# A block group of a down projection: k-tiles 12 to 15 split earlier, k-tiles 16 to 19 split later, and sixteen moves spread over the loads

## The reference, cut to what matters

```python
def swiglu(x, w_gate, w_up, w_down):
    return (jax.nn.silu(x @ w_gate) * (x @ w_up)) @ w_down

x = x + 0.5 * swiglu(rms_norm(x, ffn1_norm[layer]), ffn1_w_gate[layer], ffn1_w_up[layer], ffn1_w_down[layer])
```

## Time and profile before

| what | value |
|---|---|
| median of three runs | 2539.7 us |
| the profiled execution, own time | 2539.15 us |
| its span, first to last instruction | 2536.9 us |
| TensorE (PE) busy | 2502.3 us, 99% |
| VectorE (DVE) busy | 2055.7 us, 81% |
| ScalarE (ACT) busy | 1239.9 us, 49% |
| mean granted TensorE clock | 0.998 of full speed |

### The profile page before, as it was taken

How to read it: one execution, slowest core, us unless ns; L and a number is a source line. 1 busy time by engine, 2 the same in 40 slices (tenths; PEclk the granted TensorE clock), 3 DMA queues, 4 the chain that set the end, 5 groups by cost and what they waited for, 6 DMA issues and landing times.

```text
span 2536.9 us, 33755 instructions
## 1 busy us (share of the span) xinstructions
PE 2502.3 (99%) x12499; PEld 2128.4 (84%) x12499; DVE 2055.7 (81%) x2443; ACT 1239.9 (49%) x1692; POOL 254.6 (10%) x284
## 2 busy tenths in 40 slices
PE   8999999999999999999999999999999999999998
PEld 7888988888889888888888888888888888888887
DVE  7988758889888699975566999769988679899874
ACT  6445436664444544543225545445454437654542
POOL 0000004800000000000000000000000047200000
PEclk9999999999999999999999999999999999999999
DMA  6776432156754367553333675545766321367552
GB/s 212 166 166 141 111 96 78 34 150 158 177 114 141 118 167 169 126 137 108 100 97 111 169 167 126 138 141 132 165 135 156 100 90 42 109 157 169 125 142 87
DMA packets 493313, 331.38 MB, mean 131 GB/s; under 512 B 287968, under 2 KB 405472, under 8 KB 493152
## 3 DMA queue, kind: packets, MB, share of 16 engines
q1 hardware_dynamic: 481056, 285.19, 40.2%
q0 software_dynamic: 12096, 44.05, 9.9%
HBM read 248.68 MB, written 2.10 MB: 99 GB/s over the span
## 4 chain that ended last, share of the span: by engine, by line
PE 85%; DVE 8%; ACT 2%; issue 2%; SPq 1%; DMA 1%; POOL 1%; DVEq 0%; POOLq 0%; ACTq 0%
PE pair L594 25%; PE pair L595 25%; PE pair L596 25%; PE pair L801 3%; PE pair L802 3%; PE pair L803 3%; DVE wl L1751 2%; DVE Hl L1763 1%; PE pair L877 1%; ACT wh L1246 1%; SPq L2787 1%; PE pair L953 0%; PE pair L952 0%; DVE Df L1763 0%; DVE Dl L1763 0%
## 5 line engine op out<-in xcount | busy, mean ns | idle before, releaser
L1246 ACT ACTIVATE wh<-raw 128x1024 fp32r<-128x1024 f32 (+4 forms) x571 | 576.5, 1013 | 679.3 <-PE pair L596 534.8
L1751 DVE TENSOR_TENSOR wl<-raw,wh 128x1024 fp32r<-128x1024 f32 (+4 forms) x571 | 662.3, 1163 | 249.7 <-ACT wh L1246 248.0
L594 PE MATMUL pair<-wh,Xl 128*128 128x512 f32 (+2 forms) x976 | 374.9, 384 | 7.4 <-DVE wl L1751 7.3
L594 PE MATMUL pair<-wh,Sl 128*128 128x512 f32 x960 | 373.9, 389 | 1.0 <-DVE wl L1751 0.9
L596 PE MATMUL pair<-wh,Xh 128*128 128x512 f32 (+2 forms) x976 | 373.9, 383 | 0.0
L595 PE MATMUL pair<-wl,Xh 128*128 128x512 f32 (+2 forms) x976 | 373.8, 383 | 0.0
L596 PE MATMUL pair<-wh,Sh 128*128 128x512 f32 x960 | 373.5, 389 | 0.0
L595 PE MATMUL pair<-wl,Sh 128*128 128x512 f32 x960 | 373.5, 389 | 0.0
L1246 ACT ACTIVATE wh<-part 128x1024 fp32r<-128x1024 f32 x144 | 153.0, 1062 | 277.9 <-PE pair L596 91.2
L594 PE MATMUL pair<-Hh,wl 128*128 128x512 f32 (+1 forms) x669 | 257.9, 386 | 0.0
L595 PE MATMUL pair<-Hl,wh 128*128 128x512 f32 (+1 forms) x669 | 257.5, 385 | 0.0
(11 more groups left out here) (347 smaller groups left out, 4341.2 us busy)
## 6 DMA issues: line engine op xcount, KB each, us to landing
raw<-in_ffn_w_gate SPq DMA_DIRECT2D x120, 512.0 KB, 5.4
raw<-in_ffn_w_up SPq DMA_DIRECT2D x120, 512.0 KB, 4.3
raw<-in_ffn_w_down SPq DMA_DIRECT2D x114, 512.0 KB, 4.7
part<-raw POOLq DMA_DIRECT2D x66, 512.0 KB, 5.4
H<-H SPq DMA_DIRECT2D x288, 64.0 KB, 3.9
H<-squares SPq DMA_DIRECT2D x192, 64.0 KB, 2.1
raw<-in_c_w_in SPq DMA_DIRECT2D x24, 512.0 KB, 3.6
raw<-raw POOLq DMA_DIRECT2D x18, 512.0 KB, 9.2
```

The source lines that it names most:

```text
L594: e.matmul(o, ll, rh, start=start, stop=False, skip_group_check=again)
L1246: e.activation(part_of(n, wh), source_of(n), ACT.Copy).then_inc(whi.up(("w", n)), 1)
L1751: e.tensor_tensor(part_of(n, wl), source_of(n), part_of(n, wh).bitcast(F), ALU.subtract).then_inc(wlo.up(("w", n)), 1)
```

## The change

On ScalarE, one copy of k-tiles 12 to 15 of tokens 0 to 255 (1024 values per partition) at p of 8 takes the place of four of 512 values later; D0's high part moves ahead of c6; the high parts of k-tiles 16 to 19 stand behind those of B0 and B1. On VectorE, the low part `Al` of the same block (p of 9) and D0 (p of 11) are made inside the loop over p, D0's low part behind it, all ahead of the wait for batch 5; k-tiles 16 to 19 get their low parts at u of 4 and 5 of the group, and D3 its low part at u of 7. On SyncE, the sixteen moves of batch 5 stood as six ahead of c6's load and ten ahead of c7's; they now stand as four ahead of c6's, two ahead of c7's, and two ahead of each of the group's first five loads.

```diff
+        Al = nc.alloc_sbuf_tensor_at("Al", [128, 4, 256], R, offset=sq_at)
...
-                turned_product(a, "dA", inputs(BLOCKED, 0))
+                turned_product(a, "dA", upper)
...
# ScalarE
+                    if p == 8:
+                        w.wait_ge(mm, ("E2", s, 4))
+                        w.wait_ge(turned_in[3], ("turned", s, 3))
+                        copy(Hh0[:, BLOCKED:BLOCKED + 4, 0:256],
+                             H[:, BLOCKED:BLOCKED + 4, 0:2, :].rearrange("p k t q -> p k (t q)"), ("Ah", s))
+                w.wait_ge(dve, ("D", s, 0))
+                copy(Dh[0][:, :, :], Df[0][:, :, :], ("Dh", s, 0))
                 w.wait_ge(dve, ("h", s, 4))
                 use()
...
-                for j in (0, 3):
-                    w.wait_ge(dve, ("D", s, j))
-                    copy(Dh[j][:, :, :], Df[j][:, :, :], ("Dh", s, j))
-                for k0 in (BLOCKED, BLOCKED + 4):
-                    use()
-                    for k in range(k0, k0 + 4):
-                        hidden_high(s, k)
+                w.wait_ge(dve, ("D", s, 3))
+                copy(Dh[3][:, :, :], Df[3][:, :, :], ("Dh", s, 3))
+                use(2)
+                for k in range(BLOCKED + 4, BLOCKED + 8):
+                    hidden_high(s, k)
# VectorE, in the loop over p
+                    if p == 9:
+                        w.wait_ge(act, ("Ah", s))
+                        w.wait_ge(turned_in[3], ("turned", s, 3))
+                        tt(Al[:, :, :], inputs(BLOCKED, 0), Hh0[:, BLOCKED:BLOCKED + 4, 0:256].bitcast(F), ALU.subtract, ("Al", s))
+                    if p == 11:
+                        w.wait_ge(mm, ("xused", s))
+                        difference(0, inputs(BLOCKED, 0), inputs(BLOCKED, 256))
+                difference_low(0)
...
-                for m in (3, 5):
-                    w.wait_ge(turned_in[m], ("turned", s, m))
-                w.wait_ge(mm, ("xused", s))
+                w.wait_ge(turned_in[5], ("turned", s, 5))
                 difference(2, inputs(BLOCKED, 256), inputs(BLOCKED + 4, 256))
                 difference(1, inputs(BLOCKED, 0), Df[2][:, :, :])
                 for t in range(2):
                     add_down(t)
                 use()
-                difference(0, inputs(BLOCKED, 0), inputs(BLOCKED, 256))
                 difference(3, inputs(BLOCKED + 4, 0), Df[1][:, :, :])
                 use()
-                for j, k0 in ((2, BLOCKED), (1, BLOCKED + 2)):
-                    difference_low(j)
-                    for k in (k0, k0 + 1):
-                        hidden_low(s, k)
-                use()
-                for j, k0 in ((0, BLOCKED + 4), (3, BLOCKED + 6)):
-                    difference_low(j)
-                    for k in (k0, k0 + 1):
-                        hidden_low(s, k)
-                use()
+                difference_low(2)
+                difference_low(1)
+                use()
                 use()
                 for t in range(2, 4):
                     add_down(t)
                 for u in range(14):
+                    if u in (4, 5):
+                        for k in (2 * u - 8, 2 * u - 7):
+                            hidden_low(s, BLOCKED + 4 + k)
+                    if u == 7:
+                        difference_low(3)
# SyncE
-  (3, ((4, 0, 6), (4, 2, 2), (4, 3, 2), (4, 4, 4), (4, 5, 2))), (5, ((4, 6, 6), (4, 7, 10)))):
+  (3, ((4, 0, 6), (4, 2, 2), (4, 3, 2), (4, 4, 4), (4, 5, 2))), (5, ((4, 6, 4), (4, 7, 2), *((4, n, 2) for n in range(8, 13))))):
```

More of the change, by code:

```diff
@@ L772, in blocked, with upper, lower @@
                 a, b, d, x = pairs_of(s)
-                def inputs(k0, q0):
+                def upper(k):
+                    w.wait_ge(act, ("Ah", s))
+                    w.wait_ge(dve, ("Al", s))
+                    return Hh0[:, BLOCKED + k, 0:256], Al[:, k, :]
+                def lower(q0):
+                    k0 = BLOCKED + 4
                     def parts(k):
@@ L810, in blocked @@
                 turned_product(d, "dD", sums(0))
-                turned_product(b, "dB2", inputs(BLOCKED + 4, 256))
-                turned_product(a, "dA2", inputs(BLOCKED + 4, 0), False)
+                turned_product(b, "dB2", lower(256))
+                turned_product(a, "dA2", lower(0), False)
                 turned_product(x, "dE2", sums(3), False)
@@ L1969, in ffn, with inputs, difference, difference_low @@
                                 hidden_low(s, k)
+                def inputs(k0, q0):
+                    return H[:, k0:k0 + 4, :, :].rearrange("p k t q -> p k (t q)")[:, :, q0:q0 + 256]
+                def difference(j, x, y):
+                    w.wait_ge(dve, HERE)
+                    tt(Df[j][:, :, :], x, y, ALU.subtract, ("D", s, j))
+                def difference_low(j):
+                    w.wait_ge(act, ("Dh", s, j))
+                    tt(Dl[j][:, :, :], Df[j][:, :, :], Dh[j][:, :, :].bitcast(F), ALU.subtract, ("Dl", s, j))
                 for p in range(14):
```

## The result

| | us | |
|---|---|---|
| before | 2540.34 (2538.56 to 2541.12, 4 runs) | |
| after | 2577.52 (2574.52 to 2580.11, 4 runs) | ratio 1.0147, 95% interval 1.0129 to 1.0165 |
| forecast | 2546, range 2530 to 2556 | |

The change makes the kernel 37 us slower. The direction and the place were forecast, the size was not: 6 us were expected, and 2577.5 us lies outside the range of 2530 to 2556. The profiled execution after has a span of 2574.6 us, 37.7 more than before.

A forecast was written before the change was run, and what follows sets the result against it. VectorE's order around batch 5 was taken as the bound: 16.4 us of waits and clock go, 15.6 us of stalls and 6.8 us of low clock come, net +6.0 us, so 2546 us, range 2530 to 2556.

The forecast's parts named there:

- The waits at line 801: TensorE's waits at the block group, laid to VectorE's order around batch 5, go: 14.7 us plus 1.7 us of clock.
- The early and the late work is free: VectorE's added early work (3.4 us a stage) fits its idle time, and work moved into the group catches up: costs nothing.
- The stall falls on c6: VectorE ends c6's low part 4.82 us after its wait for batch 5, so a landing after 249.86 stalls TensorE there.
- When the last move lands: Batch 5's last move lands at 252.5 in stage 1, stalling TensorE 2.6 us in each of six stages, 15.6 us.
- the sum (+6.0): Whole kernel: 16.4 us away against 15.6 us of stalls and 6.8 us of low clock added, net +6.0 us.
- a deeper queue pays less per load: SyncE's queue: reason for taking the landing at 252.5, with 2.5 us a round from a span of 2.1 to 3.2.
- rival (c): GpSimd's additions share the DMA engines with batch 5's last moves: stall 3.9 us a stage, +17, 2557 us; chance 0.16.
- The clock: Stalls at c6 lower TensorE's granted clock in four of six stages, 1.7 us each, 6.8 us.
- a landing at 255.0: Batch 5's last move in stage 1 if each round of load and two moves takes 3.2 us, the upper end.
- the addition's 3 us: Upper bound on what one GpSimd addition sharing the DMA engines could cost batch 5's last moves.
- the landing near 249.4 us: Stage 1's lower end for batch 5's last move, if moves pass between the loads: no stall, about 2523 us.

The follow-up runs named there:

- e1: Changed kernel with batch 5's moves back at their old places, six ahead of c6's load and ten ahead of c7's: 2522.47 us, ratio 0.9936 to before.
- e8: Kernel before with only the low parts of k-tiles 16 to 19 and D3's moved back into the group, old moves' table: 2522.57 us.
- e3: Changed kernel, moves spread, but VectorE and ScalarE write the parts of c6 and c7 ahead of the wait for batch 5: 2532.41 us.
- e5b: Changed kernel with GpSimd's first two additions of weights of the block group held until batch 5 is in place: 2567.11 us.
- e5: Changed kernel with a hold on GpSimd's additions that stood only ahead of the third one, so in effect a repeat: 2578.21 us.
- e10: Changed kernel with the last ten moves of batch 5 issued by ScalarE on its own queue, SyncE issuing the loads without them: 2563.69 us.
- e12: Changed kernel with three of the group's loads ahead of the last move of batch 5 instead of four: 2558.34 us.
- e11: Changed kernel with three group loads ahead of the last move, and GpSimd's first two additions held until batch 5 is in place: 2550.09 us.
- e6: Changed kernel with two of the group's loads ahead of the last move of batch 5 instead of four: 2531.86 us.

## Why the prediction was right in place and wrong in size

- **The waits at line 801 are VectorE's, and go.** Right: 14.7 us of waits and 1.7 us of clock, 16.4 together; e1 measured 16.5. That it was VectorE, as the timelines said, and not ScalarE, as the waits view had it, is borne out by e8, which changes VectorE alone.
- **The early and the late work is free.** Right: in e1 VectorE still has 1.63 us of idle time ahead of batch 5, and no unit of the group is late.
- **The stall falls on c6, 4.82 us behind the landing.** Right: 4.81 us in stage 1 after, and e3 removes the stall by taking c6 and c7 out of the wait's way.
- **When the last move lands.** This term was mis-sized, and it is the step that failed: 15.6 us of stalls in the sum against 41.5 measured, 25.9 of the 32.7 us by which the sum (+6.0) missed the account (+38.7). I took 2.5 us for a round of load and two moves and so a landing at 252.5 in the times of before (c6 due at 254.78), a stall of 2.6 us a stage. After, c6 was due at 254.17 and VectorE went on at 254.33: in the times of before 254.94. The mean stall is 6.9 us. Two parts: the round takes about 3 us and not 2.5, also with the additions held (31.6 us of stalls in e5b against the 15.6), near the upper bound of 3.2 that I had read from the row with a load and two moves and had set aside for "a deeper queue pays less per load"; and rival (c), the additions, is real at 1.7 us a stage (41.5 against 31.6), and I left it out of the forecast. In the profiled execution stage 1 stalls least, the other five 1.1 to 3.3 us longer; e5, the same kernel to within 0.7 us, stalls 7.6 us in stage 1. So this is not a property of the stage: it goes with the last round, 3.2 us in stage 1 of the first execution, 4.6 in e5, 4.0 to 5.2 in the other five stages. What decides whether an addition hits that round is not shown. I had also misread when its transfers begin: not some 2 us after the issue at 253.37, but at 257.3, 4.0 us after (the first packet of q0, the additions' queue, in the trace before); after, it is 248.26 and 251.2.
- **The clock.** I took four drops at 1.7 us. There were six, and they cost 13.6 us, 2.3 each, so this term is 6.8 us short as well. The granted clock was low for 6.8 us at a time in stages 1, 3, 4 and 6 and for 10.2 us in 7 and 9, and what of that falls into the stall costs nothing: behind the restart it was low for 5.7, 3.5, 3.4, 5.2, 4.7 and 4.8 us. That does not go by the stall's length; stage 1 has the shortest stall and the longest low stretch behind it (to about 265, with c6 and c7 due in it). Of the stalls at c5, at c6 and in the group in all kernels here, those up to 1.6 us left the clock at full, those of 1.9 to 2.8 us did so in some cases (1.98 in stage 9 before, 2.08 in stage 6 before, 2.16 in e10, 2.76 in e12) and not in others (1.98 in stage 7 before, 2.36 in e11, 2.44 in e6), and every one from 3.0 us on lowered it.
- **The chances.** The forecast 2546 and rival (c), 2557, bracket only the lower part of what can happen: 6 x (6.9 + 2.3) - 16.4 = +39. The range stopped at a stall of 3.8 us. The working had both ends at hand: a landing at 255.0 and the addition's 3 us make 258.0, a stall of 8.1 and +42, 2582 us.

## What to carry to other kernels

When small moves with a consumer in waiting are interleaved with bulk loads, price the last landing by the round that the trace already shows for such a mix (here 3.2 us for one load and two moves), not by the bulk rate, and let the range reach as far as the upper bounds of all terms together. Put the issues that an engine will wait for ahead of the loads that nobody needs yet. And what stands behind a wait on an engine's in-order list matters more than the wait: moving two weight units ahead of it (e3) took 45 of 55 us of the loss away with the landing as late as ever.

## What the runs showed of the hardware that I had not expected

- A second queue does not take moves past loads. Eight moves of 64 KB issued from ScalarE beside SyncE's loads took 9.58 us to issue, against some 0.66 us for one undisturbed, and the last landed 8.4 us after its issue, against 2.1 us. The Trainium skill, page "DMA: Bandwidth & Descriptors", section "Rules for kernel authors", says that issuing from several engines doesn't help bandwidth since all run on the same engines. This trace agrees only in part: the loads still slow the moves down, but 307 GB/s were moved from two queues where one queue moved 236 in the same stretch. How much of that is due to one more load among the moves is not separated. It also adds that the issuing engine itself is held, ScalarE for 9.4 us, which the rule's remark on saved issue time would not lead one to expect.
- Interleaved in one queue, loads and moves cost each other more than their sum. The backlog of six moves behind c6's load drains at 0.38 us a move before (they land from 241.7 to 243.6), and the loads alone that follow land 1.3 to 1.4 us apart (five of the group's, from 252.8 to 258.2): 2.1 us for a round by that, against 3.1 mixed. From two queues, in stages 1 and 6 of e10, a load and two moves took 2.0 to 2.1 us. Why one queue does worse is not shown.
- Moves do pass a load, but by little. In stage 1 after, the first move behind the load issued at 241.46 landed at 247.2 and the load at 247.7; the first moves of the next two pairs were 0.5 and 0.9 us ahead of their loads. That is no way to the landing near 249.4 us for which such a passing would have been needed.
